# Fourteen weight pieces loaded as 120 rows and 8 rows instead of 128 rows

## The reference

```
def peer_mixer(h, w_q, sub_keys, u, v):          # h: 512 tokens x 1024
    q = (h @ w_q).reshape(B, S, 8, 2, 128)        # w_q: 1024 x 2048
    s = einsum('bshpc,hpnc->bshpn', q, sub_keys)
    ...                                           # top 16 of 16x16 candidates, 8 heads -> idx, gate
    a = einsum('tkd,td->tk', u[idx], h)           # 128 rows of u for each token
    w = gate * gelu(a)
    return einsum('tk,tkd->td', w, v[idx])        # 128 rows of v for each token
```

## Time and profile before

| | us |
|---|---|
| median of 3 runs | 2883.48 (2882.32 to 2884.63) |
| the profiled execution, its own time | 2884.08 |
| span of that execution (first to last instruction) | 2882.3 |
| PE busy | 2265.8 (79%) |
| DVE busy | 2143.5 (74%) |
| POOL busy | 1282.7 (45%) |
| ACT busy | 1072.4 (37%) |

### The profile page before, as it was taken

One profiled execution on the slowest core, in us unless ns is written; L12 is line 12 of the kernel. 1 busy time (PEld: TensorE's weight loads), 2 busy tenths in 40 slices (PEclk: granted clock), 3 DMA queues, 4 the chain that ended last, 5 costly groups with the idle time before them and its releaser, 6 DMA issues.

```text
span 2882.3 us, 23329 instructions
## 1 busy us (share of the span) xinstructions
PE 2265.8 (79%) x6572; PEld 1170.4 (41%) x6572; DVE 2143.5 (74%) x4489; ACT 1072.4 (37%) x3181; POOL 1282.7 (45%) x1029
## 2 busy tenths in 40 slices
PE   6787667976978987888687898799967788666555
PEld 4444234522534553455253455346624433222112
DVE  6888768875797667757979766686696977677776
ACT  2443324333334333632323434364332334333222
POOL 2353543544434544533543443454444334555552
PEclk9899988988999998999898999999988999887877
DMA  9999999999999999999999999999999999999995
GB/s 363 420 399 420 419 421 401 417 420 420 419 408 412 380 420 420 419 420 420 408 420 384 416 374 419 421 419 420 420 398 420 419 420 420 420 420 420 420 421 216
DMA packets 164786, 1175.37 MB, mean 408 GB/s; under 512 B 18480, under 2 KB 19888, under 8 KB 23600
## 3 DMA queue, kind: packets, MB, share of 16 engines
q0 software_dynamic: 147456, 1073.81, 90.3%
q1 hardware_dynamic: 16624, 98.24, 8.4%
q10 hardware_dynamic: 576, 1.84, 0.2%
HBM read 1171.71 MB, written 2.10 MB: 407 GB/s over the span
## 4 chain that ended last, share of the span: by engine, by line
PE 36%; DMA 35%; DVE 18%; ACT 5%; issue 4%; POOL 2%; DVEq 0%; SPq 0%; ACTq 0%; POOLq 0%
DMA slot<-in_uv,idx 35%; PE acc L933 18%; DVE slot L1648 6%; DVE X L1639 3%; PE B L687 3%; PE B L605 3%; PE M L605 2%; POOL slot L582 2%; PE M L875 2%; PE M L687 1%; PE B L875 1%; ACT diag L1158 1%; DVE SD L1275 1%; DVE top_u L1280 1%; ACT A L948 1%
## 5 line engine op out<-in xcount | busy, mean ns | idle before, releaser
L933 PE MATMUL acc<-slot,diag 128*128 128x512 f32 x2904 | 1550.7, 673 | 580.9 <-ACT diag L1158 580.1
L582 POOL DMA_INDIRECT slot<-in_uv,idx x1024 | 1282.4, 1252 | 1555.3 <-PE acc L933 1076.4
L1648 DVE CUSTOM_DVE_ANT_0 slot<-slot,HP 128x1024 f32<-128x1024 f32 x1024 | 1243.3, 1221 | 564.2 <-DMA slot<-in_uv,idx 554.4
L933 PEld LDWEIGHTS acc<-slot,diag 128*128 128x128 f32 x2904 | 571.5, 210 | 1413.0 <-ACT diag L1158 853.7
L1150 ACT ACTIVATE act_a<-a 128x1 f32<-128x1 f32 x1024 | 206.6, 202 | 1616.7 <-DVE a L1648 1615.7
L1639 DVE SCALAR_TENSOR_TENSOR X<-slot,w,X 128x1024 f32<-128x1024 f32 x297 | 380.7, 1282 | 33.4 <-ACT w L1152 33.2
L1152 ACT ACTIVATE w<-act_a,gate 128x1 f32<-128x1 f32 x1024 | 301.5, 294 | 33.2
L1158 ACT ACTIVATE diag<-cst,w 128x128 f32<-128x128 f32 x726 | 291.7, 402 | 23.8
L687 PE MATMUL B<-TT,w 128*128 128x256 f32 (+1 forms) x448 | 88.8, 354 | 0.0
L687 PE MATMUL M<-TT,w 128*128 128x256 f32 (+1 forms) x448 | 88.3, 352 | 0.0
L687 PEld LDWEIGHTS B<-TT,w 128*128 128x128 f32 x448 | 78.3, 196 | 20.7 <-issue 13.1
(11 more groups left out here) (203 smaller groups left out, 1553.5 us busy)
## 6 DMA issues: line engine op xcount, KB each, us to landing
w<-in_wq SPq DMA_DIRECT2D x28, 1024.0 KB, 9.1
slot<-in_uv,idx POOLq DMA_INDIRECT x1024, 16.9
w<-in_ple_wg SPq DMA_DIRECT2D x8, 1024.0 KB, 9.1
w<-in_w_o SPq DMA_DIRECT2D x8, 1024.0 KB, 9.1
w<-in_w_dq SPq DMA_DIRECT2D x6, 1024.0 KB, 6.9
w<-in_w_uq_nope SPq DMA_DIRECT2D x8, 768.0 KB, 8.6
w<-in_ple_wp SPq DMA_DIRECT2D x5, 1024.0 KB, 14.2
slot<-in_wq SPq DMA_DIRECT2D x4, 1024.0 KB, 15.2
```

The source lines that it names most:

```text
L582: nc.gpsimd.indirect_dma_start(out=slot[s][:], out_offset=None, in_=uv[g // NC], in_offset=bass.IndirectOffsetOnAxis(ap=idx[:, g % HPB, k: ...
L933: last = nc.tensor.matmul(acc[:, half * 512:half * 512 + 512], diag[adds_on_pe(n) % DIAGS][:], slot[s][:, D + half * 512:D + half * 512 + ...
L1648: nc.vector.tensor_tensor_reduce(out=slot[s][:, 0:D], in0=slot[s][:, 0:D], in1=HP[:, g % HPB, :], scale=1.0, scalar=0.0, op0=ALU.mult, op1 ...
```

## The change

Fourteen of the pieces are loaded by two `dma_start` instead of one: first partitions 0 to 119, then partitions 120 to 127, from the same rows of the same source. Both add 16 to the same semaphore, so PE's thresholds are counted anew: `LANDINGS[n]` is the number of transfers into that buffer up to and including piece n. The data, the places and everything that the compute engines do are the same.

```diff
+PARTED = {**{n: (120, 8) for n in (15, 17, 25, 28, 35, 38, 45, 49, 54, 58, 68, 74, 79, 84)}}
+
+def rows_of(n):
+    return PARTED.get(n, (P,))
+
+def landings():
+    counts, found = {}, []
+    for n, (where, h, _, _, there) in enumerate(HOMES):
+        if not there:
+            counts[where, h] = counts.get((where, h), 0) + len(rows_of(n))
+        found.append(counts[where, h])
+    return found
+
+LANDINGS = landings()
...
                     src = weights[name, g0 // NC][i]
-                    sp.dma_start(places[where][h][:, 0:src.shape[1]], src).then_inc(w_loaded[where][h], 16)
+                    first = 0
+                    for count in rows_of(n):
+                        part = slice(first, first + count)
+                        sp.dma_start(places[where][h][part, 0:src.shape[1]], src[part, :]
+                                     ).then_inc(w_loaded[where][h], 16)
+                        first += count
...
             def piece(name, g0, i):
-                where, h, loads, _, _ = HOMES[PIECES[name, g0, i]]
-                pe.wait_ge(w_loaded[where][h], 16 * (loads + 1))
+                n = PIECES[name, g0, i]
+                where, h, _, _, _ = HOMES[n]
+                pe.wait_ge(w_loaded[where][h], 16 * LANDINGS[n])
                 return places[where][h]
```

## The result

The kernel became slower. It takes 2941.07 us (median of 4 runs, 2940.85 to 2942.79) against 2883.07 us for the kernel before beside it (4 runs, 2882.32 to 2884.63). The ratio is 1.0202, with a 95% interval of 1.0184 to 1.0219. That is 58 us, or 4.1 us for each of the fourteen divided pieces. The forecast of 2875.0 us was off in sign, and the range (2870 to 2888) missed it.

A forecast was written before the change was run, and what follows sets the result against it. The prediction took the DMA engines to bound the kernel, with one engine always last. Sparing it was to gain 2.5 + 6 = 8.5 us from the median 2883.5, giving 2875.0 us, range 2870 to 2888.

The forecast's parts named there:

- (b): The 8 rows go one each to eight engines: 0.32 us a piece, 4.4 us on each over the kernel.
- (e): Divided pieces land at most 0.64 us later; costs nothing, as PE has no weight wait; 9 us if all showed.
- (a): In each divided piece one DMA engine is spared 8 rows, 2.54 us in most; 34.3 us in all.
- rival 3: 120 rows dealt to eight engines, 15 each: 2918 or 2890 us; sign: landings well over 9.7 us; chance 0.05.
- (c): Gathers land earlier if the spared engine is always last: 2.5 us in the last stretch plus 6 before.
- The last engine: At the gathers' end, one DMA engine ends at about 2853.3 us, 3.1 us behind the next.
- the spared one: Engine left out by a 120-row transfer, engine 15 by the skill's rule; forecast that it is last: 0.60.
- rival 2: The last engine gets one of the 8 extra rows: 2887.9 us; sign: alone for 3.4 us or more; chance 0.09.
- instruction packets: 52 and 78 packets that the engines carry beyond the even shares, taken for the cause of one engine's lateness.
- (d): SP issues 14 transfers more, 0.33 us each, behind long waits; 4.6 us if that cover were gone.
- The tail: Compute after the last gather, from 2854 us on, 29 us long, which the change does not touch.
- DVE's wait for gathers: DVE's line waits 554.4 us for gathers over the span; forecast to fall by some 8 us.

The follow-up runs named there:

- e2: Against the changed kernel, the 8-row transfers of the fourteen pieces left out, so 120 rows alone are loaded: 2922.23 us, ratio 1.0131.
- e4: Against the changed kernel, the fourteen pieces divided into 64 and 64 rows, lower and upper half of the partitions: 2929.70 us, ratio 1.0157.
- e10: Against the changed kernel, the fourteen pieces divided into 64 even and 64 odd partitions: 2884.73 us, ratio 1.0003.
- e6: Kernel before plus 40 extra transfers of 8 rows in the last 250 us, to partitions 0, 4, ... 28: 2896.60 us, ratio 1.0043.
- e12: Kernel before plus 40 extra transfers of four rows in the last 250 us, to partitions 0, 4, 8, 12: 2896.67 us, ratio 1.0048.
- e1: Against the changed kernel, the fourteen pieces in two transfers of all 128 rows, each with half of the columns: 2886.62 us, ratio 1.0004.
- e7: Kernel before plus 40 extra transfers of 8 rows in the last 250 us, to partitions 120 to 127: 2941.60 us, ratio 1.0198.

## Why the prediction was wrong

**The step that failed is the price of a moved row, in (b) and (e).** It took 0.32 us a row from the gathers, whatever partition the row lands on, and made "at most 0.64 us" on a divided piece's landing the bound, 9 us if all came to light. The rows of the trace of before that the price was taken from are those of transfers of 128 rows, where 99 of 100 gather rows took 0.324 us or less, so 0.318 us was the price of a row that nothing holds up. In the kernel after, the rows of a divided piece took a median of 0.51 us, and a third of the gather rows beside them over 0.4. The 120-row transfers of e2 land 4.1 us later than whole pieces, and in the kernel after a divided piece costs 4.1 us of the kernel's time. For an operation that no row shows (a transfer with other than 128 rows) there was no upper bound in the trace, and (b) and (e) set one from rows of another kind. The direction of (e) was right and named the place; the size was over six times too small (0.64 us a piece for 4.1), and "costs nothing" looked only at who waits for the piece, not at the gathers behind it.

The Trainium skill has the rule that the prediction didn't weigh ("SBUF — State Buffer", Door 1: The DMA port swizzle): partitions belong to 16 ports of eight, in fours 32 apart, and a transfer's bandwidth hangs on how many ports it reaches; 64 partitions from 0 on reach only eight. "DMA: Bandwidth & Descriptors" (The descriptor swizzle) adds that in a transfer of 128 partitions each engine writes one port of its own. The runs agree: e4, whose transfers would reach eight ports each, falls to 282 GB/s, and e10, whose transfers would reach all sixteen, stays at 419. By the table of ports the 8 rows at 120 to 127 lie on two ports, for eight engines, and those of e6 on eight ports; that gave 1.4 and 0.3 us. How SP deals 120 rows no run shows. If an engine gets eight neighbouring partitions, the fifteen begin on eight of the ports together, which would suit e2; but the same dealing would make e10's engines start on eight ports too, with two rows each, and e10 lost nothing. So how the 120 rows meet, and with them the 37 us of e2, stays open; what is shown is that rows are slow or not by the partitions that share a transfer.

**(a), the relief of one engine, was right in its count.** q1 has 98 packets more, 7 a piece: 15 + 8 small packets where 16 were. The long transfer lies on 15 engines (e2), so the short one on 8. This also settles rival 3 as written: the long transfer is not on eight engines with 15 rows each, which would have made q1's number the same (8 + 8). It came nearest in size (34 us) with the wrong mechanism, and its sign for being seen, landing times far above 9.7 us, came true in e2 (13.2 us; the page of the kernel after gives none) for another reason.

**(c), the gain of 8.5 us, rested on a guess that fell.** The last engine is very likely one of the first four of a short transfer (e12). That the 8 rows of a divided piece go to the same engines no run shows by itself, but the last engine wasn't the spared one: it stays alone at the end for about 4.6 us, where the forecast had it under 1. That was rival 2 (3.4 us or more), whose 4.4 us are in the right direction and lie inside the 58 where they can't be told apart. With rival 2 in the place of (c) the forecast would have been 2888 instead of 2875, still 53 us short. That instruction packets make this engine late was a guess too, and no run tries it.

**(d), the 14 issues, cost nothing that can be seen**: e1 and e10 have them too, and are at 1.0004 and 1.0003, with intervals that end at 4.3 and 3.7 us.

**The tail** stayed as predicted, and DVE's wait for gathers was the right row to watch: it rose by 64.5 us instead of falling by 8.

What the 58 us are made of: the 120 rows 37 us (e2), the 8 rows 19 us (e2 against the changed kernel; e7 gives 14 x 1.4 = 20), together 56 in the place of the 9 that (e) allowed. The other 2 us are the difference between the two medians of the kernel before, 2884.74 beside e2 and 2883.07 beside the change.

## What to carry to other kernels

A DMA share of 1.00 isn't a rate: read it with the GB/s of the same stretch. Where the DMA engines are the bound, load with all 128 partitions in one transfer, and if a tile must be divided, divide its columns (e1) or interleave its partitions (e10), which cost nothing here, and not its range of partitions (e4: 3.2 us a piece, the change: 4.1). A price per row taken from full transfers says nothing about a transfer of another shape; measure one before fourteen are built on it.

## What was not expected of the hardware

A transfer slows others more than itself: two thirds of the loss (38 of 58 us) were in the gathers' rows on q0, of which 160 of 463 took over 0.4 us beside one divided piece. A load of 64 KB in one block of eight partitions cost 1.4 us of the kernel's time, 4.4 times its 0.318 us on each engine. And two transfers of 64 rows, even and odd, were as good as one of 128, landing in a median of 9.0 us where a whole piece takes 9.1. No version here beat the kernel before; e1 and e10 equal it within 0.15%.
